# A two-block transformer kernel on one core: weight chunks loaded in halves, the scan's rotary step divided anew, and rows turned before their norm

## The chip, the cores and the metric

The kernel runs on one core of one Trainium2 chip. The time is device time in microseconds of one execution of the whole program. Lower is better. Every time below comes from the kernel before the change.

## The reference

Two transformer blocks are applied to `x` (256 rows, 1024 columns, f32). Every gemm keeps f32 accuracy.

```python
def rmsnorm(x, g): return x * rsqrt(mean(x * x) + eps) * g
# first block
h = rmsnorm(x, pre_mix_g)
aq, ak, av, hq, hf_fwd, hf_bwd, hi, hg = split(h @ w_in)      # 512, 128, 128, 5 x 512
att = axial_gqa_attention(rope(rmsnorm(aq)), rope(rmsnorm(ak)), av)
rec = hgrn2_group(hq, hf_fwd, hf_bwd, hi, hg)                 # gated scan in both directions
x = x + rmsnorm(concat(att, rec) @ w_out, post_mix_g)
h = rmsnorm(x, pre_x_g); m = rmsnorm(mem, mem_norm_g)
x = x + rmsnorm(cross_attention(h @ wq, m @ wkv) @ wo, post_x_g)
x = x + rmsnorm(conv_ffn(rmsnorm(x, pre_ffn_g)), post_ffn_g)
# second block
h = rms_norm(x, ln_mix_pre)
qa, ka, va, cq, ckv, k_rope, g_a, g_b = split(h @ w_in)
oa = differential_attention(rope(qa), rope(ka), va); y_a = rms_norm(oa) @ w_proj_a
qb = rms_norm(cq) @ w_uq; kv = rms_norm(ckv) @ w_ukv; y_b = latent_attention(...) @ w_proj_b
x = x + rms_norm((sigmoid(g_a) * y_a + sigmoid(g_b) * y_b) @ w_o)
x = x + rms_norm((silu(h2 @ w_gate) * (h2 @ w_up)) @ w_down)  # h2 = rms_norm(x)
```

## The kernel before

The program is written by hand, engine by engine, with semaphores; the order in the code is the order on each engine. `x`, the gains and all intermediates stay in SBUF, and only the weights stream.

**Weights.** A chunk is up to 8 x 512 elements for each of 128 partitions (2 MB). SyncE loads it into one of the two slots of `sb_ring` (L1377). A chunk is used in pieces of 1024 elements for each partition. ScalarE writes the rounded high part of a piece to `sb_whi` (L1563, called `ahead`), VectorE the remainder to `sb_wlo` (L2151), and TensorE multiplies three times (`products`, L542): high by high, high by low, low by high. TensorE waits for the low part of a piece. A load waits until the low parts of the whole chunk that held its slot are made, and a piece waits until its whole chunk has landed; only the very first piece has a load of its own. `sb_tahi`, `sb_talo`, `sb_tbhi` and `sb_tblo` are the high and low parts of the turned activations; `lent...hi` and `lent...lo` are further places for pieces.

**Scan.** The gated scan is computed in eight levels. At each, VectorE multiplies the queries (L2307), keeps blocks of the product of the level before under a mask (L2282), multiplies the keys (L2297), and TensorE multiplies queries by keys (L777, 32 small matmuls). Between two levels TensorE has one piece of weights to multiply. The squares of the axial attention's queries and keys are summed over each head in L2340, and GpSimd makes their factors (L1426, L1427). The rotation has two rows of blocks (r = 0, 1). For each, four multiplications by sines and cosines (L2355 to L2358 on VectorE for r = 0, L1479 on GpSimd for r = 1) are followed by two additions (L2361, L2362 on VectorE; L1483 on GpSimd).

**Norms.** Before the cross attention, ScalarE squares x (L1585), GpSimd makes the factor of each row (`rstd`), VectorE writes x times it (L2163), TensorE turns the result (L700, 16 transposes into the banks `M`, 4 to 7), and ScalarE and VectorE write high and low parts (L1594, L2173). Banks 6 and 7 were used just before by the last gemm of the memory's keys and values, and ScalarE empties them (L1642). The second block starts in the same way: `norm_rows` L2531, `turn_norm_rows`, and L1844 and L2540 for the high and low parts. There the row passes over the query columns (`qa0`, `qa1`) go first over row block 0, then over row block 1, while the end of the first block's feed-forward is still being added to x (L2522).

**Second block.** The queries and keys of the differential attention are rotated from PSUM (L2671, L2673); the latent attention's queries are rotated in `rotate_queries(0)` and `(1)`, beside the soft maxima of head 7 (`probs_da(7)`, ending with L2761).

## Time and profile before

| what | value |
|---|---|
| median of 3 runs | 910.58 us (909.86 to 911.84) |
| profiled execution | 910.87 us |
| its span, first to last instruction | 909.1 us |
| mean granted TensorE clock | 0.994 |
| TensorE matmuls busy | 887.9 us, 98% |
| VectorE busy | 613.2 us, 67% |
| ScalarE busy | 480.8 us, 53% |
| GpSimd busy | 91.2 us, 10% |

The profiled execution is 1.8 us longer than its span: what lies before the first and behind the last instruction. It is 0.3 us above the median. The ends of matmuls are modelled and overlap the next start, so that an idle time in a row of TensorE is about 0.16 us shorter than what the start of the next instruction is late by.

### The profile page before, as it was taken

To read this page: it belongs to the slowest core of one execution; us is meant where nothing else is said; L and a number is where in the kernel's file an instruction comes from. 1 tells how busy PE (TensorE), PEld (TensorE's weight loads), DVE (VectorE), ACT (ScalarE), POOL (GpSimd) and SP (SyncE) were. 2 spreads that over 40 slices of the span, in tenths; PEclk is the share of its full clock that TensorE was granted. 3 is DMA by queue.
4 is the path that set the end of the run, shared out by engine and by line. 5 is a ranking of instruction groups with operands and counts; after the bars stand their busy time and mean duration, and the time that the engine had idled before them with its cause. 6 is when DMAs were issued, how large, how long until landed. Compare 5 with 4: busy or idle time off the path is not lost.

```text
span 909.1 us, 14159 instructions
## 1 busy us (share of the span) xinstructions
PE 887.9 (98%) x5644; PEld 782.9 (86%) x5644; DVE 613.2 (67%) x960; ACT 480.8 (53%) x846; POOL 91.2 (10%) x125
## 2 busy tenths in 40 slices
PE   7999899999999999999999999999999999999997
PEld 6988797889889999999778887898878899999996
DVE  6878786484879576677856847677687773545543
ACT  5855455564477354455624366675555673325341
POOL 1413300010010000000214300012030100000000
PEclk9999899999999999999999999999999999999999
DMA  9463234454555446546416545343265563564531
GB/s 341 164 226 122 95 105 172 142 173 154 175 196 181 140 161 213 183 163 254 163 58 241 179 158 186 105 168 112 93 232 187 177 219 136 188 229 140 188 135 47
DMA packets 91697, 152.31 MB, mean 168 GB/s; under 512 B 1968, under 2 KB 52400, under 8 KB 91376
## 3 DMA queue, kind: packets, MB, share of 16 engines
q1 hardware_dynamic: 91232, 150.67, 48.0%
q8 instruction: 45, 0.74, 0.4%
q10 hardware_dynamic: 288, 0.47, 0.1%
q0 software_dynamic: 112, 0.26, 0.1%
q14 instruction: 20, 0.16, 0.0%
HBM read 150.35 MB, written 1.05 MB: 167 GB/s over the span
## 4 chain that ended last, share of the span: by engine, by line
PE 85%; DVE 7%; ACT 3%; DMA 2%; issue 2%; POOL 1%; DVEq 0%; SPq 0%; POOLq 0%; ACTq 0%
PE ps L542 75%; DMA sb_ring<-in_w_in 2%; DVE sb_wlo L2151 2%; PE ps L700 1%; ACT sb_whi L1563 1%; DVE sb_b L2307 1%; PE ps L974 1%; PE ps L878 1%; PE ps L1149 1%; PE ps L664 1%; PE ps L1325 1%; PE ps L1291 1%; ACT sb_probs L1826 1%; DVE sb_b L2297 1%; PE ps L896 0%
## 5 line engine op out<-in xcount | busy, mean ns | idle before, releaser
L2151 DVE TENSOR_TENSOR sb_wlo<-sb_ring,sb_whi 128x1024 fp32r<-128x1024 f32 (+2 forms) x169 | 203.6, 1219 | 108.1 <-ACT sb_whi L1563 107.7
L1563 ACT ACTIVATE sb_whi<-sb_ring 128x1024 fp32r<-128x1024 f32 (+2 forms) x169 | 173.9, 1045 | 106.5 <-PE ps L542 100.8
L542 PE MATMUL ps<-sb_whi,sb_tbhi 128*128 128x512 f32 (+2 forms) x296 | 116.1, 392 | 1.1 <-DVE sb_wlo L2151 1.1
L542 PE MATMUL ps<-sb_whi,sb_tblo 128*128 128x512 f32 (+2 forms) x296 | 113.3, 383 | 0.0
L542 PE MATMUL ps<-sb_wlo,sb_tbhi 128*128 128x512 f32 (+2 forms) x296 | 113.3, 383 | 0.0
L542 PE MATMUL ps<-sb_whi,sb_tahi 128*128 128x512 f32 (+1 forms) x180 | 69.9, 388 | 0.5 <-DVE sb_wlo L2151 0.5
L542 PE MATMUL ps<-sb_wlo,sb_tahi 128*128 128x512 f32 (+1 forms) x180 | 68.0, 378 | 0.0
L542 PE MATMUL ps<-sb_whi,sb_talo 128*128 128x512 f32 (+1 forms) x180 | 67.9, 377 | 0.0
L542 PEld LDWEIGHTS ps<-sb_whi,sb_tbhi 128*128 128x128 f32 x296 | 55.6, 188 | 12.4 <-DVE sb_wlo L2151 1.8
L542 PE MATMUL ps<-sb_tahi,sb_whi 128*128 128x256 f32 x216 | 61.9, 287 | 3.6 <-DVE sb_talo L2173 1.4
L542 PEld LDWEIGHTS ps<-sb_whi,sb_tblo 128*128 128x128 f32 x296 | 55.6, 188 | 10.6
L542 PEld LDWEIGHTS ps<-sb_wlo,sb_tbhi 128*128 128x128 f32 x296 | 55.7, 188 | 9.3
L2624 DVE SCALAR_TENSOR_TENSOR sb_b<-ps,sb_col,sb_b 128x255 f32<-128x255 f32 x88 | 36.1, 475 | 40.8 <-ACT sb_b L1925 40.8
L542 PE MATMUL ps<-sb_talo,sb_whi 128*128 128x256 f32 x216 | 61.1, 283 | 0.0
L542 PE MATMUL ps<-sb_tahi,sb_wlo 128*128 128x256 f32 x216 | 61.1, 283 | 0.0
L542 PE MATMUL ps<-sb_tbhi,sb_whi 128*128 128x256 f32 x208 | 60.1, 289 | 0.7 <-DVE sb_tblo L2173 0.7
L1925 ACT ACTIVATE sb_b<-ps,sb_col 128x256 f32<-128x256 f32 x44 | 22.2, 561 | 70.7 <-PE ps L542 70.7
L542 PE MATMUL ps<-sb_tblo,sb_whi 128*128 128x256 f32 x208 | 58.8, 283 | 0.0
L542 PE MATMUL ps<-sb_tbhi,sb_wlo 128*128 128x256 f32 x208 | 58.8, 283 | 0.0
L1444 POOL TENSOR_SCALAR sb_st<-sb_st 128x1 f32<-128x1 f32 x14 | 7.6, 542 | 458.0 <-ACT sb_probs L1826 458.0
L2112 ACT ACTIVATE sb_b<-ps 128x512 f32<-128x512 f32 x11 | 6.6, 596 | 79.7 <-PE ps L542 79.6
L542 PEld LDWEIGHTS ps<-sb_tahi,sb_whi 128*128 128x128 f32 x216 | 41.4, 192 | 4.6 <-DVE sb_wlo L2151 2.8
(392 smaller groups left out, 2339.3 us busy)
## 6 DMA issues: line engine op xcount, KB each, us to landing
sb_ring<-in_w_in SPq DMA_DIRECT2D x15, 2048.0 KB, 8.4
sb_ring<-in_w_up SPq DMA_DIRECT2D x22, 1024.0 KB, 5.2
sb_ring<-in_w_down SPq DMA_DIRECT2D x11, 1024.0 KB, 7.3
sb_ring<-in_w_ffn_gate SPq DMA_DIRECT2D x11, 1024.0 KB, 5.3
sb_ring<-in_w_ffn_up SPq DMA_DIRECT2D x11, 1024.0 KB, 5.3
sb_ring<-in_w_ffn_down SPq DMA_DIRECT2D x11, 1024.0 KB, 7.4
sb_ring<-in_w_xkv SPq DMA_DIRECT2D x4, 2048.0 KB, 8.5
sb_ring<-in_w_out SPq DMA_DIRECT2D x2, 2048.0 KB, 8.0
```

Of the source, the lines that this page charges most:

```text
L542: mm = pe.matmul(o, l[a_], r[b_], start=(start and n == 0), stop=(stop and n == 2), skip_group_check=not check)
L664: mm = pe.transpose(bank[b][:, j * P:(j + 1) * P], src[:, r, k * P:(k + 1) * P], ident)
L700: mm = pe.transpose(bank[b][:, j * S + r * P:j * S + (r + 1) * P], src[:, r, k * P:(k + 1) * P], ident)
L878: mm = pe.matmul(o[part:part + w, j * S + q0:(j + 1) * S], v[:, kt, c:c + w], pT[:, kt * S + q0:(kt + 1) * S], start=(kt == 0), stop=(kt = ...
L974: mm = pe.matmul(o, xqT[:, 2 * h + kt, r * P:(r + 1) * P], xkT[:, 2 * h + kt, 0:n], start=(kt == 0), stop=(kt == 1))
L1149: pe.matmul(bank[M[i]][:, r * S:r * S + n], qaT[d, h, r * P:(r + 1) * P], kaT[d, h, 0:n], start=(r == 0), stop=False, skip_group_check=True)
L1291: pe.matmul(bank[M[i]][:, r * S:r * S + n], qnT[:, 2 * p + i, q], knT[:, 2 * p + i, 0:n], start=(r == 0), stop=False, skip_group_check=True)
L1325: mm = pe.matmul(bank[M[2]][:, i * S + kt * P:(i + 1) * S], vb[:, kt, h * P:(h + 1) * P], probsT[:, i, kt * S + kt * P:(kt + 1) * S], star ...
L1563: act.activation(piece_pair(m)[0], src, ACT.Copy).then_inc(s("hi_done"), 1)
L1925: act.activation(conv[g][:, 2 * j + c, :], bank[banks.at[key][0]][:, c * S:(c + 1) * S], ACT.Identity, bias=COL[:, COL_CONVB + at:COL_CONV ...
L2151: dve.tensor_tensor(low, pieces[m][1], high.bitcast(F32), ALU.subtract).then_inc(s("lo_done"), 1)
L2624: dve.scalar_tensor_tensor(dst, src, COL[:, at:at + 1], dst, ALU.mult, ALU.add).then_inc(banks.release(key) if last and c else s("ffn1_tap ...
```

## The change

The change has five parts.

1. Full chunks are loaded in two halves, each with its own semaphore, and each waits for the low parts of its half of the slot alone. A few smaller chunks stay whole.
2. The scan's rotation: VectorE makes all multiplications of both row blocks (`rope1_mul`), GpSimd all additions. The sums of squares and the first four multiplications stand ahead of level 3, the others ahead of levels 4 and 5. Two pieces of `aq` stand between the two first multiplications of the queries.
3. At the cross attention x is turned as it is, and the squares are made behind the high parts. The factor enters as the scale of the exponential, and VectorE multiplies the maxima by it. The transposes go row block by row block.
4. At the second block's entry x is turned as it is (`turn_sums`), the two turns of row block 0 stand two of its four parts earlier in the last down projection of row block 1, and the order on ScalarE and VectorE changes. The factor enters later: in the rotations, the latent squares, the values and the gates.
5. `rotate_queries(1)` stands ahead of `probs_da(7)`.

```diff
@@ chunk @@
-            raw_halves[name] = (2 * slot, 2 * slot + 1)
-            chunks.append((name, [(raw[name], w[0:k * P, c0:c0 + n])], k, n))
+            if k * n < SLOT or k < 4:
+                halves = (2 * slot,) if k * n <= HALF else (2 * slot, 2 * slot + 1)
+                parts = [(halves, [(v3(ring, slot * SLOT, k, n), src)])]
...
@@ block.sync, load @@
-                for before in raw_before[name]:
-                    sp.wait_ge(*lo_done(pieces_of[before][-1]))
+                for j, (_, loads) in enumerate(chunks[index[name]][1]):
+                    for before in raw_before[name, j]:
+                        sp.wait_ge(*lo_done(last_of[before]))
...
@@ block.tensor, cross attention @@
-            turn_norm("pre_x_g")
+            for m in range(4):
+                banks.take(pe, f"pre_x_g.{m}", M[m], 2)
+            for r in range(R):
+                for m in range(4):
+                    if m % 2 == 0:
+                        pe.wait_ge(s("w_out_added"), 2 * r + m // 2 + 1)
+                    for j in range(2):
+                        k = 2 * m + j
+                        mm = pe.transpose(bank[M[m]][:, j * S + r * P:j * S + (r + 1) * P],
+                                          x[:, r, k * P:(k + 1) * P], ident)
+                    if r == R - 1:
+                        mm.then_inc(banks.fill(f"pre_x_g.{m}"), 1)
...
@@ block.tensor, second block's entry @@
-            last_down(1, lambda: turn_norm_rows("ln_mix_pre_2", 0, 0, M[0]))
-            turn_norm_rows("ln_mix_pre_2", 0, 1, M[2])
+            last_down(1, {(0, 1): turn_second(0, 0, M[0]), (1, 0): turn_second(0, 1, M[2])})
...
@@ block.gpsimd @@
-            pool.wait_ge(s("rope1_mul"), 4)
+            for r in range(R):
+                zp, tp = (v.rearrange("p (i two) -> p i two", two=2)
+                          for v in (qkv[:, r, 0:640], rtmp[:, r * 640:(r + 1) * 640]))
+                pool.wait_ge(s("rope1_mul"), 4 * (r + 1))
...
@@ block.scalar, cross attention @@
+                                           scale=stats["pre_x_g"][1][:, r:r + 1],
...
@@ block.scalar, second block's entry @@
-            ahead_of("qa0", 3)
-            norm_rows_of(norm, "ffn1_added", 0)
             ahead_of("qa0", 4)
-            tiles_hi(norm, hT2, gain, 0, 0)
+            for half in range(2):
+                tiles_hi(norm, hT2, gain, 0, half)
             for c in range(2):
                 post_rows_of("ffn1", f"ffn1.{2 * c + 1}", c, 1)
-            tiles_hi(norm, hT2, gain, 0, 1)
+            norm_rows_of(norm, "ffn1_added", 0)
             ahead_of("qa1", 2)
...
@@ block.vector, scan @@
-            for n in range(4):
+            for n in range(3):
                 next_level(n)
...
-            next_level(4)
...
+                for tab, q, n in zip(tables, (slice(0, 512), slice(512, 640)), (8, 2)):
+                    dve.tensor_tensor(heads(dst[:, q]), heads(z[:, q]), table(tab[:, r, :], n), ALU.mult
+                                      ).then_inc(s("rope1_mul"), 1)
...
-            rope1_turn(0)
+            for part in range(2):
+                rope1_mul(0, part)
+            next_level(3)
+            rope1_mul(1, 0)
+            next_level(4)
+            rope1_mul(1, 1)
             next_level(5)
...
@@ block.vector, cross attention @@
+                            dve.wait_ge(s("pre_x_g_rstd"), 1)
+                            dve.tensor_tensor(top, top, stats["pre_x_g"][1], ALU.mult).then_inc(s(f"{name}_max"), 1)
...
@@ block.vector, rotate @@
+                    dve.scalar_tensor_tensor(t, zu, rstd2(r), sines, ALU.mult, ALU.mult).then_inc(s("rope2_mul"), 1)
+                    i = dve.scalar_tensor_tensor(out, zu, rstd2(r), cosines, ALU.mult, ALU.mult)
...
@@ block.vector, heads of the differential attention @@
+                    if h == 7:
+                        rotate_queries(1)
                     probs_da(h)
...
-                if h == 7:
-                    rotate_queries(1)
```

VectorE, in the scan's levels, before: the rotation of row block 0 stands whole between the keys of level 4 and the piece ahead of level 5 (`sb_tsq`, `sb_tsk`, `sb_tcq` and `sb_tck` are the sines and cosines).

```order
L2151 TENSOR_TENSOR sb_wlo<-sb_ring,sb_whi 128x1024 [waits hi_done]
L2355 TENSOR_TENSOR sb_b<-sb_b,sb_tsq 128x512 [waits qk1_sq]
L2356 TENSOR_TENSOR sb_b<-sb_b,sb_tsk 128x128
L2357 TENSOR_TENSOR sb_b<-sb_b,sb_tcq 128x512
L2358 TENSOR_TENSOR sb_b<-sb_b,sb_tck 128x128
L2361 TENSOR_TENSOR sb_b<-sb_b 128x320 [waits dve_step]
L2362 TENSOR_TENSOR sb_b<-sb_b 128x320
L2151 TENSOR_TENSOR sb_wlo<-sb_ring,sb_whi 128x1024 [waits hi_done]
L2307 TENSOR_TENSOR sb_b<-sb_b 128x32x16 [waits scan_q,filled5,filled4]
L2307 TENSOR_TENSOR sb_b<-sb_b 128x32x16
L2282 COPY_PREDICATED sb_b<-sb_masks,ps 128x256 [waits emptied4,filled4]
L2282 COPY_PREDICATED sb_b<-sb_masks,ps 128x256 [waits emptied5,filled5]
```

The same engine after, from the sums of squares on; the cuts leave out the work of the levels 3 and 4.

```order
L2379 TENSOR_REDUCE sb_st<-sb_b 128x10 [waits qk1_squares] x2
L2395 TENSOR_TENSOR sb_b<-sb_b,sb_tsq 128x512 [waits qk1_sq]
L2395 TENSOR_TENSOR sb_b<-sb_b,sb_tsk 128x128
L2395 TENSOR_TENSOR sb_b<-sb_b,sb_tcq 128x512 [waits qk1_sq]
L2395 TENSOR_TENSOR sb_b<-sb_b,sb_tck 128x128
L2188 TENSOR_TENSOR sb_wlo<-sb_ring,sb_whi 128x1024 [waits hi_done]
...
L2188 TENSOR_TENSOR sb_wlo<-sb_ring,sb_whi 128x1024 [waits hi_done]
L2395 TENSOR_TENSOR sb_b<-sb_b,sb_tsq 128x512 [waits qk1_sq]
L2395 TENSOR_TENSOR sb_b<-sb_b,sb_tsk 128x128
...
L2188 TENSOR_TENSOR sb_wlo<-sb_ring,sb_whi 128x1024 [waits hi_done]
L2395 TENSOR_TENSOR sb_b<-sb_b,sb_tcq 128x512 [waits qk1_sq]
```

The first four multiplications moved ahead of level 3, the two additions are gone, and row block 1's multiplications stand ahead of the levels 4 and 5, two by two.

TensorE ahead of the cross attention's query gemm, before: each bank has a wait of its own, and is filled by its own four transposes. The cut repeats this for bank 6.

```order
L700 MATMUL ps<-sb_col,sb_b 128x128 [waits emptied4,pre_x_g_scaled]
L700 MATMUL ps<-sb_col,sb_b 128x128 x3
L700 MATMUL ps<-sb_col,sb_b 128x128 [waits emptied5]
...
L700 MATMUL ps<-sb_col,sb_b 128x128 [waits emptied7]
L700 MATMUL ps<-sb_col,sb_b 128x128 x3
L542 MATMUL ps<-sb_tbhi,sb_whi 128x256 [waits emptied4,emptied0,lo_done]
```

The same place after; the cut leaves out the other groups of four, which wait for `w_out_added` alone.

```order
L992 MATMUL ps<-sb_col,sb_x 128x128 [waits emptied7,emptied6,w_out_added,emptied5,emptied4]
L992 MATMUL ps<-sb_col,sb_x 128x128 x3
L992 MATMUL ps<-sb_col,sb_x 128x128 [waits w_out_added]
...
L560 MATMUL ps<-sb_tbhi,sb_whi 128x256 [waits emptied4,emptied0,lo_done]
L560 MATMUL ps<-sb_tblo,sb_whi 128x256
```

The first transpose now waits until all four banks are empty, and since row block 0 goes through all banks first, bank 4 is full only with the tenth transpose.

ScalarE at the second block's entry, before (`filled4`, `filled6`: turned rows of block 0; `filled5`, `filled7`: the last down projection of row block 1; `sb_x`: the squares of x).

```order
L1563 ACTIVATE sb_whi<-sb_ring 128x1024 [waits piece_used,weights_in2] x2
L1826 ACTIVATE sb_probs,sb_st<-sb_x 128x512 [waits ffn1_added] x2
L1563 ACTIVATE lent8hi<-sb_ring 128x1024 [waits piece_used,weights_in2]
L1844 ACTIVATE sb_tbhi<-ps,sb_col 128x128 [waits filled4]
L1844 ACTIVATE sb_tbhi<-ps,sb_col 128x128 x3
L1826 ACTIVATE sb_probs,sb_st<-ps 128x512 [waits filled5]
L1826 ACTIVATE sb_probs,sb_st<-ps 128x512 [waits filled7]
L1844 ACTIVATE sb_tbhi<-ps,sb_col 128x128 [waits filled6]
L1844 ACTIVATE sb_tbhi<-ps,sb_col 128x128 x3
L1563 ACTIVATE lent9hi<-sb_ring 128x1024 [waits piece_used,weights_in0]
L1563 ACTIVATE lent3hi<-sb_ring 128x1024 [waits piece_used,weights_in0]
L1826 ACTIVATE sb_probs,sb_st<-sb_x 128x512 [waits ffn1_added] x2
```

The same place after.

```order
L1593 ACTIVATE sb_whi<-sb_ring 128x1024 [waits piece_used,weights_in2]
L1593 ACTIVATE sb_whi<-sb_ring 128x1024 [waits piece_used,weights_in3]
L1593 ACTIVATE lent8hi<-sb_ring 128x1024 [waits piece_used,weights_in3]
L1877 ACTIVATE sb_tbhi<-ps,sb_col 128x128 [waits filled4]
L1877 ACTIVATE sb_tbhi<-ps,sb_col 128x128 x3
L1877 ACTIVATE sb_tbhi<-ps,sb_col 128x128 [waits filled6]
L1877 ACTIVATE sb_tbhi<-ps,sb_col 128x128 x3
L1859 ACTIVATE sb_probs,sb_st<-ps 128x512 [waits filled5]
L1859 ACTIVATE sb_probs,sb_st<-ps 128x512 [waits filled7]
L1859 ACTIVATE sb_probs,sb_st<-sb_x 128x512 [waits ffn1_added] x2
L1593 ACTIVATE lent9hi<-sb_ring 128x1024 [waits piece_used,weights_in0]
L1593 ACTIVATE lent3hi<-sb_ring 128x1024 [waits piece_used,weights_in0]
```

The squares of x of row block 0 moved from ahead of the turned rows to behind the squares of the down projection of row block 1. GpSimd's order is the same in both kernels: it makes the factors of the feed-forward's row block 0, of x's row block 0, of the feed-forward's row block 1, and of x's row block 1, in this order.

## Rows read from the trace of the kernel before

**Rows 1.** The page, busy time and share of the span by engine.
```profile
PE 887.9 (98%) x5644; PEld 782.9 (86%) x5644; DVE 613.2 (67%) x960; ACT 480.8 (53%) x846; POOL 91.2 (10%) x125
```

**Rows 2.** TensorE's timeline: start, us, engine, line, operation, count, [idle before <-releaser].
```profile
15.83 0.39 PE L542 MATMUL ps<-sb_tahi,sb_whi 128*128 128x256 f32 x1 [0.89 <-DVE sb_wlo L2151]
...
53.95 0.50 PE L542 MATMUL ps<-sb_whi,sb_tahi 128*128 128x512 f32 x1 [0.49 <-DVE sb_wlo L2151]
...
97.73 1.97 PE L777 MATMUL ps<-sb_b 128*64 128x64 f32 x32 [3.48 <-DVE sb_b L2282]
...
193.68 1.91 PE L700 MATMUL ps<-sb_col,sb_b 128*128 128x128 f32 x16
...
196.26 0.36 PE L542 MATMUL ps<-sb_tbhi,sb_whi 128*128 128x256 f32 x1 [0.67 <-DVE sb_tblo L2173]
...
448.59 0.47 PE L542 MATMUL ps<-lent2hi,sb_tbhi 128*128 128x512 f32 x1 [0.58 <-DVE sb_tblo L2540]
...
457.06 0.50 PE L542 MATMUL ps<-lent3hi,sb_tbhi 128*128 128x512 f32 x1 [1.41 <-DVE lent3lo L2151]
...
489.64 0.50 PE L542 MATMUL ps<-sb_whi,sb_tbhi 128*128 128x512 f32 x1 [0.83 <-DVE sb_wlo L2151]
...
614.91 0.36 PE L542 MATMUL ps<-sb_tahi,sb_whi 128*128 128x256 f32 x1 [1.22 <-DVE sb_b L2673]
```

**Rows 3.** Windows: length, busy of five engines, granted clock, DMA share, GB/s.
```profile
94.00:98.00 4.00, 0.52 (x7) 0.30 (x7) 4.00 (x6) 0.00 (x0) 3.92 (x3) 0.85 0.40 91
98.00:105.00 7.00, 7.00 (x50) 5.89 (x48) 5.92 (x9) 2.44 (x4) 0.09 (x1) 0.60 0.65 250
...
455.00:465.00 10.00, 8.59 (x42) 6.78 (x42) 8.13 (x19) 2.71 (x9) 0.00 (x0) 1.00 0.40 131
```

**Rows 4.** VectorE's timeline, where the levels of the scan stand.
```profile
76.72 1.23 DVE L2151 TENSOR_TENSOR sb_wlo<-sb_ring,sb_whi 128x1024 fp32r<-128x1024 f32 x1 [2.87 <-ACT sb_whi L1563]
77.86 1.29 DVE L2307 TENSOR_TENSOR sb_b<-sb_b 128x512 f32<-128x512 f32 x2
...
82.07 1.54 DVE L2340 TENSOR_REDUCE sb_st<-sb_b 128x10 f32<-128x640 f32 x2
...
88.86 0.68 DVE L2355 TENSOR_TENSOR sb_b<-sb_b,sb_tsq 128x512 f32<-128x512 f32 x1
...
92.65 2.31 DVE L2151 TENSOR_TENSOR sb_wlo<-sb_ring,sb_whi 128x1024 fp32r<-128x1024 f32 x1
94.88 2.34 DVE L2307 TENSOR_TENSOR sb_b<-sb_b 128x512 f32<-128x512 f32 x2
```

**Rows 5.** GpSimd's timeline beside it.
```profile
86.10 3.54 POOL L1427 TENSOR_TENSOR sb_st<-sb_st,sb_neghalf 128x20 f32<-128x20 f32 x1
...
95.35 2.73 POOL L1483 TENSOR_TENSOR sb_b<-sb_b 128x320 f32<-128x320 f32 x2
```

**Rows 6.** ScalarE's timeline at the start and at the cross attention.
```profile
13.45 2.96 ACT L1563 ACTIVATE sb_whi<-sb_ring 128x1024 fp32r<-128x1024 f32 x3 [0.89 <-DMA sb_ring<-in_w_in]
...
186.88 0.63 ACT L1585 ACTIVATE sb_b<-sb_x 128x512 f32<-128x512 f32 x1
...
193.88 0.60 ACT L1642 ACTIVATE sb_b<-ps 128x512 f32<-128x512 f32 x1 [0.76 <-PE ps L542]
```

**Rows 7.** The chain that ended last, at the first key chunk: start, us, what.
```profile
479.39 7.85 DMA sb_ring<-in_w_in
```

**Rows 8.** The page's DMA part: queue, KB each, median us to landing.
```profile
sb_ring<-in_w_in SPq DMA_DIRECT2D x15, 2048.0 KB, 8.4
...
sb_ring<-in_w_ffn_gate SPq DMA_DIRECT2D x11, 1024.0 KB, 5.3
```

**Rows 9.** VectorE, then GpSimd, at the second block's entry.
```profile
451.36 1.41 DVE L2522 SCALAR_TENSOR_TENSOR sb_x<-sb_b,sb_st,sb_x 128x512 f32<-128x512 f32 x2
...
452.95 1.00 POOL L1444 TENSOR_SCALAR sb_st<-sb_st 128x1 f32<-128x1 f32 x1 [2.67 <-ACT sb_probs L1826]
```

**Rows 10.** VectorE, at the query rotation of the latent attention.
```profile
614.01 0.42 DVE L2671 TENSOR_TENSOR sb_b<-ps,sb_ropes 128x256 f32<-128x256 f32 x1
```

212 lines of the change are left out of this document (108 added, 104 removed).

## The prediction, made before the changed kernel was run

> **What bounds the kernel now.** I read the busy times first: TensorE multiplies for 887.9 us of a span of 909.1 [rows 1], so that 21 us are left to it in which it does nothing. No engine can gain anything but in these gaps, in the clock, or by taking matmuls away, and the change takes none away: transposes and matmuls keep their number. I then went through TensorE's timeline for starts that are late. Eight gaps are touched by the change [rows 2]: 15.83 (idle 0.89), 53.95 (0.49), 97.73 (3.48), 196.26 (0.67), 448.59 (0.58), 457.06 (1.41), 489.64 (0.83) and 614.91 (1.22); in each the releaser is VectorE. The sum of the idle times is 9.57 us; with 0.16 each for the modelled ends it is 10.85 us of late starts. Last I read the clock in windows: it is granted at 0.85 from 94 to 98 and at 0.60 from 98 to 105 [rows 3], that is half speed (1.2 instead of 2.4 GHz) for most of 7 us, right behind the gap of 3.48 in which TensorE had been busy 0.52 of 4 us. It costs 7 x (1 - 0.60) = 2.8 us. The window from 455 to 465, which holds the gap of 1.41, has clock 1.00 [rows 3]. So the largest object is the gap at 97.73 with what follows: 3.64 late and 2.8 slow.
>
> **Scan's rotation: -2.7, and -2.75 by the clock.** VectorE sits idle for 2.87 us before 76.72 and from there works without a stop until the masks of level 5 release TensorE at 97.73 [rows 4]. In that stretch it does three things that the change touches: the sums of squares, 1.54 (1.46 without the overlap); the rotation of row block 0, from 88.86 to 92.65, 3.79; and it runs slower while GpSimd rotates row block 1: the low part at 92.65 takes 2.31 against 1.23 at 76.72, the pair of query multiplications 2.34 against 1.29 [rows 4], 2.13 together. Sum 7.4. After the change the sums and the four multiplications of row block 0 (1.73, from 88.86 to the first addition) stand in the idle 2.87: 3.19 in 2.87 leaves 0.3. The multiplications of row block 1 cost 1.73 ahead of the levels 4 and 5. GpSimd still adds, two pairs of 2.73 [rows 5]; the trace shows what a pair does to VectorE: between 95.35 and 97.2 the query multiplications ran for 1.87 us and lost 1.05, 0.56 of each us. Over 2.73, with mask and PSUM work in between that I take as unhurt, I put 1.25 for each pair, 2.5. GpSimd's first pair stands behind the factors, whose power takes 3.54 and ends at 89.64 [rows 5], 6.0 after the sums' end at 83.61; with sums that end at 75.3 the pair starts at about 81, so both pairs fall inside the stretch. After: 0.3 + 1.7 + 2.5 = 4.5, that is 2.9 less than 7.4. TensorE waits 3.64 now, so about 0.8 to 0.95 stay and 2.7 goes. With a gap under that of 457.06, which left the clock at 1.00, the clock should not fall, and I take 2.75 back. Bounds: additions that cost VectorE nothing take all 3.64; additions that stop it for their whole time leave 0.3 + 1.7 + 5.46 = 7.5, no gain.
>
> The Trainium skill, "SBUF — State Buffer", section "Who interferes with whom", calls the port that VectorE and GpSimd share an exclusive lock: the loser stands for the whole of the other's instruction. By that rule VectorE would lose up to 5.46 us and the gap would stay at 3.6. The row of the query multiplications (1.05 lost in 1.87) bears it out in part.
>
> **Halves: -0.75, -0.65, -1.0.** At the start ScalarE waits 0.89 for a DMA before 13.45 [rows 6], the load of the other three quarters of the first chunk. After the change the second piece comes with a quarter; ScalarE goes on at 12.56, its high part is done at 13.6, the low part at about 14.95 behind the low parts of the rows, against 14.8 at which TensorE wants it: 0.15 to 0.3 of 1.05 stay, -0.75. At 53.95 the gain comes from the two `aq` pieces set between the first query multiplications: one of these, 1024 elements wide, no longer stands ahead of the low part. I take it at a low part's 1.23 [rows 4], the same width, more than the 0.65 of lateness, so all of it goes; the second multiplication is not wanted for some us. At 489.64 the first key chunk is late: its load starts at 479.39 and takes 7.85 [rows 7]. Half chunks of 1024 KB land in 5.3 where 2048 KB take 8.4 [rows 8]: 3 us sooner, against 1.0 of lateness, -1.0. Elsewhere no TensorE wait ends at a load, so halves are worth nothing there; ten more issues on SyncE's queue are 0.4 us each and lie beside 8 us loads. Bound: if the second half lands later than the whole did, 0.5 us at one or two places.
>
> **Cross attention: +1.65.** VectorE's four multiplications go, but no gap stood on them: the first transpose started at 193.68, with the last gemm's end [rows 2]. What releases it now is ScalarE's copy out of banks 6 and 7, 193.88 + 0.60 [rows 6]: start 194.5. The 16 transposes take 1.91 [rows 2], 0.11 to 0.12 each, and bank 4 is full with the tenth instead of the fourth: 195.75. Before, ScalarE began its high parts at 194.4 and the gemm started at 196.26, 1.9 later. The same 1.9 behind 195.75 is 197.7: +1.4. The squares of x, moved behind the high parts, are four of 0.63 with a read behind each [rows 6], 2.6 us ahead of the third query piece: its high part is done at 202.4, its low part at 203.65, wanted at 203.5: +0.25. Cover of the maxima's extra multiplication (0.25 a head): more than 1 us in which the probabilities wait for their turn. Bounds: +1.1, if VectorE's low parts follow at once, and +2.5, if the squares delay one more piece.
>
> **Second block's entry: -0.6.** The rows are turned two parts of the down projection sooner, and need no factor: the lateness at 448.59 (0.74) goes. The one at 457.06 (1.57) stood on the second row block: the additions to x at 451.36, 1.41 [rows 9], then its squares, then GpSimd's factor from 452.95, 2 us [rows 9], then VectorE's norm, and the piece `lent3` behind it. Norm and factor leave this path. But GpSimd now makes the factor of row block 0's x before that of the feed-forward's row block 1, and ScalarE makes those squares last, until about 450.15: factor of x by 451.2, factor of the feed-forward by 452.4, additions to x until 453.85, `lent3` low part at 455.0, which TensorE wants at 453.35. So about 1.7 stays late where 1.57 was; 0.74 - 0.13 = 0.6. **Rotation of the latent queries: -1.35.** TensorE waits at 614.91 for a bank that the rotation empties, and this starts at 614.01 [rows 10]. Ahead of the probabilities it runs while VectorE waits for ScalarE's exponential, by 613.1. All 1.38 goes; the probabilities come 0.7 later, and the next turn has more than that.
>
> Later factors cost VectorE 0.06 for each rotation, 1 us in all, and 0 on the path, as VectorE is busy 67% [rows 1].
>
> **Sum.** 2.7 + 2.75 + 0.75 + 0.65 + 1.0 + 0.6 + 1.35 - 1.65 = 8.15. The profiled execution took 910.87, so 902.7; it lay 0.3 above the median, and I forecast a median of 902.5.
>
> **Rivals.**
> (a) Levels unchanged, chance 0.10: VectorE stands for the whole of GpSimd's additions, or the level after is late in their place. For it: 2.31 against 1.23. Against it: the pair lost only 1.05 of 1.87. It keeps 3.6 of lateness and 2.8 of clock: 902.5 + 5.45 = 908.
> (b) The clock falls once at a new place, chance 0.12. At the cross attention TensorE has a gap of 0.8 (193.7 to 194.5), 1.8 us of transposes, and one of 1.5 to 2. If this counts as one long gap, it costs what the other cost, 2.8: 905.3.
> (c) All of the scan and more, chance 0.10: the additions cost nothing, the entry's inversion is hidden: 0.9 and 1.5 less, 900.3.
> (d) Slower than before, chance 0.05: on GpSimd the factor of x's row block 0 waits for squares that ScalarE makes after the down projection's squares, and everything of row block 1 waits behind it. I price it at 1.7. It decides if each of the four links (squares, factor, addition, low parts) is 2 us longer than I read them, so that TensorE stands 9 us and comes back at half clock: 902.5 + 8 + 2.8 = 913. Against it: each link has a row within 2 us.
> (e) Halves and entry bring nothing, chance 0.13: the slot's second half sets the time, and the first half's load shares the queue. Then 2.35 less gain: 904.9.
>
> **How the numbers follow.** The forecast as it stands has 0.50; (c), (e) and (b) lie on its two sides. The range from 899.5 to 906.5 holds the forecast, (b), (c) and (e), 0.85 less its tails; (a) and (d) lie outside. No change within 0.2% (908.8 to 912.4), about what a measurement can tell of this kernel, needs (a) with one more loss: 0.06. Slower by over 0.2%: (d), 0.05. Faster: 0.89.
>
> **What would show it.** In the profile after: no gap over 1 us between 94 and 98 and clock 1.00 from 98 to 105; VectorE without an idle of 2 us before level 3, GpSimd's additions in two pairs from about 81; TensorE's first query matmul of the cross attention 4.0 us behind the end of the last key and value gemm instead of 2.6; a gap of about 1.5 at the second row pass of `qa0`, behind the additions to x; no gap at the first key chunk or at the latent queries' third piece. It would be wrong if the clock fell anywhere else, or if a gap over 1 us stood at a place not named here.

## The result, and the profile after

The changed kernel takes 905.83 us in the median of five executions (four of them from 905.65 to 907.21) against 911.72 for the kernel before in the same comparison. The ratio is 0.9947 with a 95% interval of 0.9933 to 0.9961, so it is faster by 0.53%. A second comparison gave 905.81 against 910.24, ratio 0.9948 (0.9935 to 0.996). One execution of the changed kernel (971.64 us at a mean granted clock of 0.849), and one of the kernel without the entry part below (1162.45 us at 0.704), are left out. The profile read here is of an execution of 906.1 us at 0.998.

The forecast was 902.5, a gain of 8 us or 0.9%. The time lies inside the range, at its upper end, and the size was wrong: 4.4 us came by the medians of the second comparison, 4.7 to 4.8 by the ratios.

First the busy times of the changed kernel. They answer to [rows 1]: TensorE's matmuls are the same in number, and 1.2 us shorter in sum.

```profile
PE 886.7 (98%) x5644; PEld 781.2 (86%) x5644; DVE 610.9 (68%) x958; ACT 482.5 (53%) x846; POOL 91.0 (10%) x123
```

TensorE's timeline of the changed kernel follows, at the places that answer to [rows 2]. L802, L560 and L788 are the former L777, L542 and L763 (the last product of the scan).

```profile
15.39 0.39 PE L560 MATMUL ps<-sb_tahi,sb_whi 128*128 128x256 f32 x1 [0.15 <-DVE sb_wlo L2188]
...
95.04 0.28 PE L802 MATMUL ps<-sb_b 128*64 128x64 f32 x2 [1.34 <-DVE sb_b L2319]
...
110.24 0.38 PE L788 MATMUL ps<-sb_b 128*128 128x128 f32 x1 [1.17 <-DVE sb_b L2344]
...
191.02 0.41 PE L992 MATMUL ps<-sb_col,sb_x 128*128 128x128 f32 x2 [0.89 <-ACT sb_b L1673]
...
194.23 0.35 PE L560 MATMUL ps<-sb_tbhi,sb_whi 128*128 128x256 f32 x1 [1.28 <-DVE sb_tblo L2210]
...
453.26 0.50 PE L560 MATMUL ps<-lent9hi,sb_tbhi 128*128 128x512 f32 x1 [1.70 <-DVE lent9lo L2188]
```

Of the gaps of before, 3.48 at 97.73 is 1.34 at 95.04 (0.15 more is late at 86.84), and those at 53.95, 489.64 and 614.91 are gone. The cross attention has two gaps, 0.89 and 1.28, where 0.67 stood. At the second block's entry one of 1.70 stands where there were two of 0.58 and 1.41. New is 1.17 at 110.24, ahead of the scan's last product. In the kernel before TensorE came there at 114.23 without a wait.

The windows that answer to [rows 3], of the changed kernel:

```profile
94.00:98.00 4.00, 2.96 (x40) 2.60 (x41) 3.54 (x6) 1.51 (x3) 0.00 (x0) 1.00 0.84 262
98.00:105.00 7.00, 7.00 (x78) 6.58 (x77) 5.05 (x8) 3.69 (x7) 0.00 (x0) 1.00 0.45 152
```

The granted clock is 1.00 in both, as forecast. Two of the signs that the prediction named against itself came true: a gap over 1 us is left between 94 and 98, and one stands at a place that it did not name, 110.24.

To see where time came and went I compared the start of one and the same TensorE instruction in both traces. A negative number says how much earlier the changed kernel is there.

```
start before   start after   earlier by   what lies between this row and the one above
 53.95          53.25         -0.70       -0.14 at the start, -0.56 at the aq pieces
 97.73          95.04         -2.69       rotation
103.64          98.32         -5.32       clock at 1.00 instead of half speed
114.23         110.24         -3.99       +1.32, new gap at the last product
116.13         112.42         -3.71       +0.28, behind it
196.26         194.23         -2.03       +1.68, cross attention
457.06         454.75         -2.31       -0.28, second block's entry
489.64         486.45         -3.19       -0.88, first key chunk
614.91         610.25         -4.66       -1.47, latent queries
last                          -4.72
```

### The profile page after: what moved, and what is told of

Its sections match the earlier page's. It is cut to its first block, busy times and chain, and to the rows that moved or that the text cites. A ratio compares the mean times of both kernels' runs of the same rounds, so it can differ in the third digit from the quotient of the medians.

```text
span 969.8 us, 14209 instructions
## 1 busy us (share of the span) xinstructions
PE 956.3 (99%) x5644; PEld 813.8 (84%) x5644; DVE 613.3 (63%) x958; ACT 483.1 (50%) x846; POOL 84.3 (9%) x123
## 4 chain that ended last, share of the span: by engine, by line
PE 96%; DVE 2%; ACT 1%; DMA 1%; issue 1%; POOL 0%; DVEq 0%; POOLq 0%; SPq 0%; ACTq 0%
PE ps L560 84%; PE ps L725 1%; PE ps L802 1%; PE ps L903 1%; PE ps L1010 1%; PE ps L682 1%; PE ps L1186 1%; PE ps L1328 1%; PE ps L1362 1%; PE ps L1208 1%; DMA sb_x<-in_x 1%; PE ps L921 0%; PE ps L947 0%; PE ps L933 0%; PE ps L1048 0%
## 5 line engine op out<-in xcount | busy, mean ns | idle before, releaser
L2188 DVE TENSOR_TENSOR sb_wlo<-sb_ring,sb_whi 128x1024 fp32r<-128x1024 f32 (+2 forms) x169 | 203.2, 1213 | 125.4 <-ACT sb_whi L1593 125.1
L1593 ACT ACTIVATE sb_whi<-sb_ring 128x1024 fp32r<-128x1024 f32 (+2 forms) x169 | 173.9, 1044 | 126.0 <-PE ps L560 125.2
L560 PE MATMUL ps<-sb_whi,sb_tbhi 128*128 128x512 f32 (+2 forms) x296 | 123.4, 417 | 0.0
L560 PE MATMUL ps<-sb_whi,sb_tblo 128*128 128x512 f32 (+2 forms) x296 | 121.1, 409 | 0.0
L560 PE MATMUL ps<-sb_wlo,sb_tbhi 128*128 128x512 f32 (+2 forms) x296 | 120.8, 408 | 0.0
L560 PE MATMUL ps<-sb_whi,sb_tahi 128*128 128x512 f32 (+1 forms) x180 | 73.2, 406 | 0.0
L560 PE MATMUL ps<-sb_whi,sb_talo 128*128 128x512 f32 (+1 forms) x180 | 71.6, 398 | 0.0
L560 PE MATMUL ps<-sb_wlo,sb_tahi 128*128 128x512 f32 (+1 forms) x180 | 71.5, 397 | 0.0
L560 PEld LDWEIGHTS ps<-sb_whi,sb_tblo 128*128 128x128 f32 x296 | 56.7, 192 | 15.5
L560 PEld LDWEIGHTS ps<-sb_whi,sb_tbhi 128*128 128x128 f32 x296 | 57.0, 193 | 14.9 <-issue 1.2
L560 PEld LDWEIGHTS ps<-sb_wlo,sb_tbhi 128*128 128x128 f32 x296 | 57.1, 193 | 13.7
L560 PE MATMUL ps<-sb_tahi,sb_whi 128*128 128x256 f32 x216 | 63.9, 296 | 1.3 <-DVE sb_talo L2210 1.3
L560 PE MATMUL ps<-sb_talo,sb_whi 128*128 128x256 f32 x216 | 63.5, 294 | 0.0
L560 PE MATMUL ps<-sb_tahi,sb_wlo 128*128 128x256 f32 x216 | 63.4, 294 | 0.0
L560 PE MATMUL ps<-sb_tbhi,sb_whi 128*128 128x256 f32 x208 | 61.7, 296 | 1.2 <-DVE sb_tblo L2210 1.2
L560 PE MATMUL ps<-sb_tbhi,sb_wlo 128*128 128x256 f32 x208 | 60.6, 291 | 0.0
L560 PE MATMUL ps<-sb_tblo,sb_whi 128*128 128x256 f32 x208 | 60.4, 290 | 0.0
L560 PEld LDWEIGHTS ps<-sb_tahi,sb_whi 128*128 128x128 f32 x216 | 43.5, 202 | 1.7 <-DVE sb_wlo L2188 1.6
```

The costliest lines, as they stand in the source:

```text
L560: mm = pe.matmul(o, l[a_], r[b_], start=(start and n == 0), stop=(stop and n == 2), skip_group_check=not check)
L1593: act.activation(piece_pair(m)[0], src, ACT.Copy).then_inc(s("hi_done"), 1)
L2188: dve.tensor_tensor(low, pieces[m][1], high.bitcast(F32), ALU.subtract).then_inc(s("lo_done"), 1)
```

## The experiments

### The parts one by one

**The changed kernel again.** Nothing is edited.

> The changed kernel again, for a profile at full clock. Prediction's terms: the gap at 97.73 has shrunk from 3.48 to under 1 us of idle and the clock is 1.00 from 98 to 105; the first query matmul of the cross attention comes about 4.0 us behind the last key and value gemm; a gap of about 1.5 us stands behind the second block's entry; no gap at the first key chunk and none at the latent queries. The measured gain of about 5 us instead of 8.2 leaves 3 us open: either the levels gave only half (theory B: over 2 us of idle left at a level, or clock under 0.9 somewhere), or the cross attention and the entry cost more (theory A: their gaps together exceed 6 us against the 3.5 of before).

It took 905.81. Theory A put the missing time in the cross attention and the entry. Their gaps with the clock's return are near the forecast: the starts give +1.68 for +1.65 and -0.28 for -0.6. Theory B comes closer, though not in its form: the levels kept less than 2 us, and the clock is up, but 1.6 us went again at 110.24 and just behind.

**Without the scan part.** The hunks of the scan on VectorE, ScalarE and GpSimd are taken back:

```diff
+            for n in range(4):
+                next_level(n)
...
+            next_level(4)
...
+            rope1_turn(0)
             next_level(5)
```

> The changed kernel with the scan's rotation and order as before. Theory A (the scan part gives all of 5.4 with the clock, 2.7 + 2.75): 905.8 + 5.4 = 911.2. Theory B (the scan part gives only half): 908.5.

The median is 910.48, 4.7 more than with the part. TensorE's timeline and the windows of this kernel:

```profile
98.53 0.48 PE L802 MATMUL ps<-sb_b 128*64 128x64 f32 x4 [3.48 <-DVE sb_b L2325]
```

```profile
98.00:105.00 7.00, 6.47 (x45) 5.43 (x46) 5.92 (x11) 2.10 (x3) 0.89 (x1) 0.57 0.45 138
```

The gap and the slow stretch are back. Its executions differ, though. At mean clocks of 0.993 they take 910.5 to 910.8; at 0.997 and 0.999 they take 908.46 and 908.71, only 2.8 above the kernel with the part. So the part itself is worth about 2.8, as in theory B, and what the slow executions lose comes to about 2 more. Not all of that is the scan's: the profiled execution also ran at 0.50 from 12 to 15 us (see the last section), and by the starts of TensorE's instructions this cost it 1.0 us or more by 33 us. About 1 us is left for the slow stretch behind the gap, a first sign that its price is not the 2.75 of the prediction.

**Without the cross attention part, and without the halves.** The first kernel turns scaled rows again, the second loads whole chunks:

```diff
-            for m in range(4):
-                banks.take(pe, f"pre_x_g.{m}", M[m], 2)
...
+            turn_norm("pre_x_g")
```

> The changed kernel with the cross attention's norm as before (rows scaled before they are turned). Prediction's term: 905.8 - 1.65 = 904.2. Theory A, cross attention costs about twice that: 902.5 to 903. If turning x as it is is worth something or nothing: 905.8 or above.

> The changed kernel with whole chunks. Prediction's terms: 905.8 + 0.75 (start) + 1.0 (first key chunk) = 907.6. Rival (e), halves bring nothing: 905.8. If the clock falls behind the gaps that come back: 910.

904.03 and 907.41. The cross attention part costs 1.8 (forecast 1.65) and the halves bring 1.6 (forecast 1.75). By TensorE's starts 0.8 of the 1.6 is at the first key chunk, which is late again without halves, as in [rows 7]:

```profile
487.27 0.51 PE L542 MATMUL ps<-sb_whi,sb_tbhi 128*128 128x512 f32 x1 [0.61 <-DVE sb_wlo L2170]
```

The start does not bear out its term of 0.75. These are the rows for the gap of [rows 2] at 15.83, first in another execution of the kernel before (the third of those under "The kernel before again"), then in the changed kernel without halves:

```profile
15.41 0.39 PE L542 MATMUL ps<-sb_tahi,sb_whi 128*128 128x256 f32 x1 [0.23 <-DVE sb_wlo L2151]
...
15.60 0.39 PE L542 MATMUL ps<-sb_tahi,sb_whi 128*128 128x256 f32 x1 [0.22 <-DVE sb_wlo L2170]
```

With whole chunks the gap is 0.22 to 0.23 here, and it was 0.89 in the profile that the prediction read. Of seven profiles with the order of before, three have 0.89 to 0.91, one 0.64 and three 0.21 to 0.26; the changed order has 0.15 or 0.16 where its clock is full at the start. So most of this gap belongs to some executions and not to the kernel.

**Without the early rotation, and without the entry part.**

```diff
                     ahead(first_gate + 3 * h + 3)
-                    if h == 7:
-                        rotate_queries(1)
                     probs_da(h)
```

> The changed kernel with the latent queries' second rotation back behind the probabilities of head 7. Prediction's term: 905.8 + 1.35 = 907.15. Rival, the stall is hidden by the halves or by the shifted schedule: 905.8.

> The changed kernel with the second block's entry as before (rows scaled by their factor before they are turned). Prediction's term: 905.8 + 0.6 = 906.4. By the shifts of TensorE's starts in the traces (0.3 gained over the entry): 906.1. With the old order of ScalarE's squares the inversion on GpSimd is gone too, so both could be even: 905.8.

907.38 and 906.46: 1.6 (forecast 1.35) and 0.65 (forecast 0.6). The gap at the latent queries is back at its old size. So taking out any of these four parts gives the forecast size within 0.25 us, and most of what is missing lies in the scan.

### What stands behind the gaps that are left

**GpSimd's order at the entry.** Both factors of the feed-forward come first:

```diff
             for r in range(R):
                 rstd_rows("ffn1", r)
+            for r in range(R):
                 rstd_rows("ln_mix_pre_2", r)
```

> The changed kernel, with GpSimd making the factors of the feed-forward's two row blocks first and those of x behind them. If the gap of 1.7 idle at 453.26 stands on GpSimd's order (factor of x's row block 0 ahead of the feed-forward's row block 1), the additions to x begin 1.3 to 1.6 us earlier and the time falls from 905.8 to 904.3. Rival, it stands on ScalarE's squares or VectorE's low parts themselves: 905.8.

903.82, a gain of 2.0. In the changed kernel VectorE waits for GpSimd ahead of the additions to x; with the edit it does not, and the additions start at 447.70 instead of 450.65. VectorE's timeline of the changed kernel, then of the edited one:

```profile
446.98 1.28 DVE L2547 TENSOR_TENSOR sb_b<-ps,sb_rowg 128x512 f32<-128x512 f32 x2
450.65 1.41 DVE L2555 SCALAR_TENSOR_TENSOR sb_x<-sb_b,sb_st,sb_x 128x512 f32<-128x512 f32 x2 [2.39 <-POOL sb_st L1484]
451.99 1.22 DVE L2188 TENSOR_TENSOR lent9lo<-sb_ring,lent9hi 128x1024 fp32r<-128x1024 f32 x1
```

```profile
446.51 1.28 DVE L2548 TENSOR_TENSOR sb_b<-ps,sb_rowg 128x512 f32<-128x512 f32 x2
447.70 1.41 DVE L2556 SCALAR_TENSOR_TENSOR sb_x<-sb_b,sb_st,sb_x 128x512 f32<-128x512 f32 x2
449.03 1.22 DVE L2189 TENSOR_TENSOR lent9lo<-sb_ring,lent9hi 128x1024 fp32r<-128x1024 f32 x1
```

The additions stand 2.95 us sooner (this execution was 0.5 ahead already before them), of which the gap of 1.70 used what it could. This is the inversion that the prediction named, and it cost the entry part most of what it could have gained: 2.0, against the 0.65 that the part brought.

**Turns bank by bank.**

```diff
+            pe.wait_ge(s("w_out_added"), 2 * R)
             for m in range(4):
                 banks.take(pe, f"pre_x_g.{m}", M[m], 2)
-            for r in range(R):
-                for m in range(4):
+                for r in range(R):
```

> The changed kernel, x still turned as it is at the cross attention, but bank by bank, as the scaled rows were turned before: banks 4 and 5 need not wait for ScalarE's copy out of 6 and 7, and bank 4 is full with the fourth transpose. If the loss of 1.8 us is the order of the transposes alone: 905.8 - 1.7 = 904.1, as with the old norm. If the squares behind the high parts hold a part of it: 904.5 to 905.3. If the missing norm on VectorE is worth something by itself: under 903.8.

904.12, a gain of 1.7: the whole loss of the part. TensorE's timeline of this kernel:

```profile
189.90 1.91 PE L990 MATMUL ps<-sb_col,sb_x 128*128 128x128 f32 x16
192.48 0.35 PE L560 MATMUL ps<-sb_tbhi,sb_whi 128*128 128x256 f32 x1 [0.67 <-DVE sb_tblo L2207]
```

The first transpose follows the gemm at once, and the gap ahead of the query gemm is the 0.67 of before [rows 2]. Missing work on VectorE was worth nothing by itself: with the loss gone the time is that of the old norm (904.03). The squares behind the high parts cost no more than 0.1, where the prediction had 0.25 for them; the order alone cost 1.7, where it had 1.4.

**Queries first at the last level.** VectorE made the low part of a piece ahead of the last multiplication of the queries, though this piece is used only behind the product:

```diff
-                ahead(reached[f"level{n}"] + 1)
+                if n < 7:
+                    ahead(reached[f"level{n}"] + 1)
                 if 0 < n < LEVELS:
                     double_queries(n - 1)
                 if n != LEVELS - 1:
                     keep_level(n)
+                ahead(reached[f"level{n}"] + 1)
```

> The changed kernel, with the last multiplication of the queries (for the product at 110.24) ahead of the piece that is wanted only behind this product. If the gap of 1.2 idle at 110.24 is this queue order and ScalarE's chain before the piece: 905.8 - 1.3 = 904.5. If the product waits for something else too (masks, keys, blocks): less than 0.3 gained.

904.58, a gain of 1.2. VectorE's timeline of the changed kernel shows the wait; L2188 is the low part, L2344 the queries.

```profile
107.75 1.23 DVE L2188 TENSOR_TENSOR sb_wlo<-sb_ring,sb_whi 128x1024 fp32r<-128x1024 f32 x1 [2.29 <-ACT sb_whi L1593]
108.90 1.29 DVE L2344 TENSOR_TENSOR sb_b<-sb_b 128x512 f32<-128x512 f32 x2
```

VectorE sits 2.29 us for ScalarE's high part, makes the low part (1.23), and only then the queries, for which TensorE waits from 108.91 to 110.24. With the edit the queries are made from 105.10 on and the product starts at 108.56 without a wait.

**Queries first from level 5 on.** The same edit with `n < 5`.

> The changed kernel, with queries and masks ahead of the piece at the levels from 5 on. If the idle 1.3 at 95.04 stands on VectorE waiting 1.25 us for ScalarE's high part and then making the low part (1.93) ahead of the queries, the gap goes, and with the one at 110.24 the time is 905.8 - 1.3 - 1.4 = 903.1. Rival, the products wait for their keys (made behind the masks) or the piece behind the product is now late: the first gap is only traded, 904.5 as with the last level alone.

902.84, a gain of 3.0: by the starts 1.4 at 95.04, and 1.6 at 110.24 and just behind it. ScalarE's and VectorE's timelines of the changed kernel ahead of 95.04:

```profile
88.30 1.16 ACT L1687 ACTIVATE sb_b<-sb_b 128x512 f32<-128x512 f32 x2 [3.09 <-DVE sb_b L2334]
89.36 1.07 ACT L1673 ACTIVATE sb_b<-ps 128x512 f32<-128x512 f32 x2
90.31 2.01 ACT L1593 ACTIVATE sb_whi<-sb_ring 128x1024 fp32r<-128x1024 f32 x2
```

```profile
91.41 1.93 DVE L2188 TENSOR_TENSOR sb_wlo<-sb_ring,sb_whi 128x1024 fp32r<-128x1024 f32 x1 [1.25 <-ACT sb_whi L1593]
93.26 1.28 DVE L2344 TENSOR_TENSOR sb_b<-sb_b 128x512 f32<-128x512 f32 x2
94.46 0.76 DVE L2319 COPY_PREDICATED sb_b<-sb_masks,ps 128x256 f32<-128x256 int32 x2
```

ScalarE copies keys from 88.30 (L1687), takes two banks (L1673), and only then makes the high part (L1593). VectorE is idle for 1.25, makes the low part, and then the queries and masks that TensorE waits for. The edit does not take this wait away; it puts the queries and masks ahead of it. The prediction replayed VectorE without this wait.

**GpSimd's additions cut short.** Each addition treats 4 pairs of 320, so a part of the rotation is left out:

```diff
-                    pool.tensor_tensor(zp[:, :, a_], zp[:, :, a_], tp[:, :, b_], ALU.add).then_inc(...)
+                    pool.tensor_tensor(zp[:, 0:4, a_], zp[:, 0:4, a_], tp[:, 0:4, b_], ALU.add).then_inc(...)
```

> The changed kernel; GpSimd's four additions of the scan's rotation are cut to 4 of 320 pairs (a part of the rotation is left out). VectorE's instructions beside them, 1.68 for 1.22, 2.12 for 1.29 and 1.93 for 1.22, go back to their own length: 2.0 us. The gap at 95.04 falls from 1.5 late to about 0.8, since the wait of 1.25 for ScalarE takes up the first pair's part; the time is 905.8 - 0.7 to - 1.5, so 904.3 to 905.1. Rival, the exclusive lock costs nothing here: 905.8.

903.87, a gain of 1.9, more than the 0.7 to 1.5 expected. VectorE's timeline of the changed kernel beside GpSimd's additions, then the first of its two query multiplications by itself:

```profile
82.62 1.68 DVE L2188 TENSOR_TENSOR sb_wlo<-sb_ring,sb_whi 128x1024 fp32r<-128x1024 f32 x1 [0.28 <-ACT sb_whi L1593]
84.23 2.12 DVE L2344 TENSOR_TENSOR sb_b<-sb_b 128x512 f32<-128x512 f32 x2
...
84.23 1.52 DVE L2344 TENSOR_TENSOR sb_b<-sb_b 128x512 f32<-128x512 f32 x1
```

GpSimd's four additions in the changed kernel, one by one:

```profile
82.21 1.02 POOL L1513 TENSOR_TENSOR sb_b<-sb_b 128x320 f32<-128x320 f32 x1
83.18 2.01 POOL L1513 TENSOR_TENSOR sb_b<-sb_b 128x320 f32<-128x320 f32 x1
90.23 1.03 POOL L1513 TENSOR_TENSOR sb_b<-sb_b 128x320 f32<-128x320 f32 x1 [5.04 <-DVE sb_b L2395]
91.21 1.04 POOL L1513 TENSOR_TENSOR sb_b<-sb_b 128x320 f32<-128x320 f32 x1
```

VectorE with the additions cut, at the same instructions:

```profile
82.33 1.23 DVE L2188 TENSOR_TENSOR sb_wlo<-sb_ring,sb_whi 128x1024 fp32r<-128x1024 f32 x1 [0.28 <-ACT sb_whi L1593]
83.47 1.29 DVE L2344 TENSOR_TENSOR sb_b<-sb_b 128x512 f32<-128x512 f32 x2
...
89.81 1.23 DVE L2188 TENSOR_TENSOR sb_wlo<-sb_ring,sb_whi 128x1024 fp32r<-128x1024 f32 x1 [1.25 <-ACT sb_whi L1593]
```

1.68 becomes 1.23, 2.12 becomes 1.29, 1.93 (above) becomes 1.23 at 89.81: 2.0 us, where the prediction put 2.5. VectorE's instructions share 3.4 us with GpSimd's two pairs, so VectorE lost 0.6 of each shared us. The single rows show how the time is shared: whichever instruction starts later stands until the other has ended, and loses that time less about 0.14. VectorE's low part of 82.62 meets an addition that ends at 83.23 and takes 0.45 longer; the next addition starts at 83.18, inside that low part, which ends at 84.30, and takes 2.01 instead of 1.03; the query multiplication of 84.23 meets it until 85.19 and takes 1.52 instead of 0.68; the low part of 91.41 meets an addition until 92.25 and takes 0.70 longer. In the kernel before it is the same: the low part of 2.31 at 92.65 [rows 4] meets a GpSimd multiplication until 93.87 and takes 1.08 longer.

The Trainium skill, "SBUF — State Buffer", section "Who interferes with whom", has the shared port as an exclusive lock and says that issue order decides who blocks; the trace agrees in all four of these meetings. VectorE's loss is smaller than the overlap because GpSimd was the later one in one of them, with 1.1 us shared.

By the starts the time fell by 1.6 at 95.04, where TensorE is no longer late at all, and by 0.4 at the last product. Contention took 2.0 us of VectorE's time and the wait for ScalarE 1.25; part of their sum was slack. To close the gap at 95.04 it is enough to take away the contention, with the wait of 1.25 still standing at 89.81, or to move the queries ahead of that wait.

**Three edits together.**

> The changed kernel with three edits: GpSimd's factors of the feed-forward first, the cross attention's turns bank by bank, queries first from level 5 on. If the gaps are independent, the gains add: 905.8 - 2.0 - 1.7 - 2.7 = 899.4. If work that comes sooner meets the next late chain, as at 110.24: 900 to 902.

900.5 in the median, 898.94 the fastest; ratio to before 0.9888 (0.9872 to 0.9903). The median lies in the band of the second expectation, but not for its reason: in the profiled execution the starts add up to what single gains give (-1.5 at 95.04, -1.6 at the last product, -1.7 and -1.9), and 1.0 is lost at the start, where it had half clock from 12 to 15. The other two at its time have its mean clock of 0.997, and the fastest has 0.998 and lies 0.5 below the additive 899.4; that they differ in the same stretch is likely, but they have no profile. This is the fastest version of the study. In its profile no gap of TensorE over 0.7 us stands behind the first 12 us.

### What the clock was worth

**The kernel before again.** Nothing is edited; three single executions, each with its profile.

> The kernel before again, for a profile of an execution in which the clock does not fall at 98 to 105. Theory (the clock's 2.75 was mostly hidden): where the mean clock is 0.998 the gap of 3.5 at 97.7 is still there, the stretch behind it runs at 1.00, and a new gap of 1.3 to 2 us stands at the last product (about 111 to 112); the span is 908, 1 us under the first profile's. Rival (the clock was worth all of it): no new gap, and a span of 906.3.

> The same once more, since the clock differs from execution to execution: at 0.993 or 0.994 the stretch is slow and there is no gap at the last product; at 0.998 the gap is there. Theory and rival as for the run ahead of it.

> The kernel before, one look. If it falls at 0.998: the stretch at 98 to 105 at 1.00, the span 908, and a gap of about 1.8 us somewhere behind it; if at 0.994, it repeats the first profile.

910.84 and 910.46 at 0.994 repeat the first profile. The third, 909.49 at 0.996, has a window from 98 to 105 at 0.76 instead of 0.60, and no new gap. None was at 0.998. By TensorE's starts the third gained 1.1 us in the faster stretch and kept 0.9 of it behind the last product.

The many executions of the kernel before that stand beside these experiments, about seventy, say the same without a profile. Nineteen of them at a mean clock of 0.998 took 909.5 to 910.1 us, 909.7 in the median; eighteen at 0.994 took 910.2 to 911.3, 910.6 in the median. A mean clock lower by 0.004 is 3.6 us of granted clock over 909 us, and it goes with 0.9 us of time. A stretch of 7 us at 0.60 alone would take 0.003 from the mean, so that an execution at 0.998 can't hold it. The prediction thus also took back a loss that many executions of the kernel before do not have.

**The kernel before, queries first at the last level.** The edit of above with `n < 7`.

> The kernel before with the last multiplication of the queries ahead of the piece that is wanted behind the last product. Theory: in executions with the full clock the hidden chain is gone and the time falls by 1.3, from 909.7 to 908.4; in those with the clock lost nothing is gained (910.5 to 911.7), so the two kinds lie up to 3 us apart instead of 1 to 2. Rival: the clock is worth all of its 2.75 in the kernel before already, and this edit gains nothing in any execution.

910.8 against 910.35, ratio 1.0002 (0.9993 to 1.0011): nothing, and its one execution at 0.998 took 909.5, not 908.4. The expected gain did not come, and this run alone speaks against the theory. It has no profile at 0.998, so what that execution waited for stays open.

**The kernel before, kept busy.** TensorE gets 13 matmuls into the gap. Their output is never read:

```diff
             def level(n):
+                if n == 6:
+                    for _ in range(13):
+                        pe.matmul(bank[M[3]][:, 0:512], hT1[0][:, 0, 0:P], hT1[0][:, 0:2, :].rearrange(...),
+                                  start=True, stop=True)
```

> The kernel before with 13 more matmuls of 512 columns (their result is not used) in TensorE's gap ahead of 97.73, which fill some 2.8 of 3.6 us. If the activity holds the clock up: 1.00 from 98 to 105. Theory (the half clock hid a late chain): then a new gap of 1.5 to 2 us stands ahead of the last product, and the time falls only to about 909.6, as in the executions of before at 0.998. Rival: the clock's 2.75 comes back whole: 907.7. If the clock falls all the same: 910.5 to 911.7.

> The same with the last multiplication of the queries ahead of the piece behind it. Theory: with the clock up the gap ahead of the last product goes, 909.6 - 1.3 = 908.3. If the edit gains nothing here too (as in the kernel before by itself), what stands there is another wait than in the changed kernel: 909.6, and its row names it.

The first took 909.83 against 910.89, ratio 0.9992 (0.9983 to 1.0001), so that no gain is clear of noise. TensorE's timeline and window of this kernel:

```profile
94.06 3.11 PE L746 MATMUL ps<-sb_tahi 128*128 128x512 f32 x13
97.77 0.45 PE L781 MATMUL ps<-sb_b 128*64 128x64 f32 x8 [0.60 <-DVE sb_b L2286]
...
113.08 1.16 PE L767 MATMUL ps<-sb_b 128*128 128x128 f32 x8 [1.31 <-DVE sb_b L2311]
```

```profile
98.00:105.00 7.00, 7.00 (x78) 6.30 (x75) 5.92 (x9) 2.40 (x4) 0.12 (x1) 1.00 0.64 243
```

The clock is 1.00 and the instruction of 103.64 comes 2.62 us earlier, nearly all of what the windows of [rows 3] said. At 113.08 TensorE stands 1.31 us, and of 2.62 only 1.07 is left at the end. The second kernel, with the queries first, took 908.7 (ratio 0.9977, 0.9969 to 0.9986). Its rows at the last product:

```profile
111.61 1.95 PE L767 MATMUL ps<-sb_b 128*128 128x128 f32 x16
113.88 1.09 PE L700 MATMUL ps<-sb_col,sb_b 128*128 128x128 f32 x8 [0.32 <-DVE sb_b L2381]
```

The last product starts without a wait, a gap of 0.32 follows, and 2.10 is left. So in the kernel before the half clock hid a chain on VectorE and ScalarE, and the queue order is most of it. With TensorE kept busy the edit of order is worth 1.1. Without, where the clock is down in most executions, it is worth nothing in the median; that it would be worth 1.1 there too once the clock is up is not shown, since the one execution at 0.998 did not have it.

## Why the prediction was wrong in size

**Right.** The halves in sum, the cross attention's loss, the entry with its inversion and the early rotation were all sized within 0.3 us, from the waits that end last. Inside them two small terms had no effect: 0.75 for the start and 0.25 for the squares. The clock stayed at 1.00 behind the smaller gap. Rival (b), a fall of the clock at the cross attention, did not occur; nor did (a), (c), (d) or (e). That the time lies inside the range is luck: the range reached so far for (b) and (e), and the missing time has another cause.

**The step that failed: "so about 0.8 to 0.95 stay and 2.7 goes" and "I take 2.75 back".** Both are in the scan's term, 5.45 in sum and 6.1 with the `aq` pieces. The clock's stretch did give 2.63 back (from -2.69 to -5.32), but 1.60 of it was gone by 116.13, since TensorE then stood before the last product. The price of a slow stretch was read as (1 - clock) times its length. That is what TensorE's own work gains, and it holds for the end only if what TensorE needs next is ready that much earlier. The check was open in the trace of before: TensorE came to the last product at 114.23, and VectorE's queries for it were made from 112.33 on, so they could not have served an arrival 2.7 us sooner unless they moved with it. These are VectorE's rows of the kernel before:

```profile
111.19 1.23 DVE L2151 TENSOR_TENSOR sb_wlo<-sb_ring,sb_whi 128x1024 fp32r<-128x1024 f32 x1 [2.91 <-ACT sb_whi L1563]
112.33 1.29 DVE L2307 TENSOR_TENSOR sb_b<-sb_b 128x512 f32<-128x512 f32 x2
```

Here L2151 waits 2.91 us for ScalarE, and L2307 are the queries, done at 113.6, 0.6 us ahead of TensorE. With the clock held up the queries came only 0.6 sooner, so that TensorE could start the product 1.2 sooner and not 2.6. The prediction named this kind of thing in no rival.

**The smaller miss in the same term.** 1.65 stayed late (1.50 at 95.04, 0.15 before it) instead of 0.85. Contention was less than I put (2.0 for 2.5). VectorE's wait of 1.25 for ScalarE's high part was not in the replay at all, because before the change VectorE was busy in that moment and ScalarE's lateness did not show; nor was one of 0.28 at 82.62. The bound of 5.46 took the exclusive lock as if VectorE were always the one that waits; by the rows it is whichever starts later.

**The start.** 0.75 and 0.65 were forecast up to 53.95, and 0.70 came. The `aq` pieces gave 0.56 of it. The wait of 0.89 is down to 0.15, but 0.44 was left of that at 15.39, as the turns ahead of it began 0.3 later than in the first profile, and 0.14 at 33.10. The term was read from one execution, and as shown above the gap of 0.89 is not there in others of the same kernel. Measured against that first profile, the profiles of the changed order with full clock at the start are 0.12 to 0.64 ahead at 33.10, the one without halves 0.22, and the other six with the order of before lie from 0.24 behind to 0.41 ahead: the term is no larger than what single executions differ by. The halves also brought 40 more issues on SyncE's queue (144 for 104), where the prediction had ten; no TensorE gap goes back to them.

**The sum.** -0.7 (start and `aq`), -2.0 (rotation), -2.6 + 1.6 (clock and what it hid), +1.7, -0.3, -0.9, -1.5: 4.7, against the forecast 8.15. Taking parts out one by one gives 4.7, -1.8, 1.6, 1.6 and 0.65, which is 6.7 and more than the whole of 4.4, in part because without the scan part the clock was down in most executions and that part is charged with it, the stretch at the start included. Of the 3.4 that are missing from the forecast, 1.75 are the clock's return, 0.7 the rotation, 0.7 the start with the `aq` pieces and 0.3 the entry. Two sums of the prediction are slightly off, with no weight in the result: 7.4 less 4.5 leaves 0.74 of the 3.64 late, not 0.8 to 0.95, and rival (c) comes to 900.1.

## What to carry to other kernels

When a term speeds up one engine, by clock or by a closed gap, follow the engines that feed it to the next two or three points where they meet, and subtract what they can't deliver sooner; a slow engine hides lateness that no wait in the trace shows. Look in each in-order queue for work that is not wanted yet standing ahead of work that is: three edits of order, with no instruction less, gave here as much again as the whole change. When work leaves a path, replay every engine that supplies the one you relieved, not that one alone.
